# The sample's attention A made in 18 steps inside the gate stage, and one gate tile moved with it

## The reference, cut to what matters

```python
k_all = concatenate([cache_a_k, ka]); v_all = concatenate([cache_a_v, va])     # 2048 + 64 keys
logits = einsum(q, k_all) * 128 ** -0.5 + bias_a[t5_bucket(s_pos - t_pos)] + mask
oa = softmax(logits) @ v_all
m = sigmoid(ga) * ((oa * silu(za)) @ w_br_a) + sigmoid(gb) * ((ob * silu(zb)) @ w_br_b)
y = rmsnorm(x + m @ w_out, final_g)
```

## Time and profile before

| | us |
|---|---|
| median of 3 runs | 3204.95 (3204.02 to 3206.44) |
| profiled execution, its own time | 3202.53 |
| span of that execution | 3200.8 |
| TensorE busy in the span | 3049.3 (95%) |
| mean granted TensorE clock | 0.979 |
| `gates`, first to last product | 1473.7 to 2113.2 |
| last product of `attend_merge` to first of `merge_a` | 2492.6 to 2588.5 |

### The profile page before, as it was taken

The page is one execution under the profiler, slowest core; times in us unless marked ns, Lnnn a source line. Parts: engine busy times, 40 slices in busy tenths (PEclk is TensorE's granted clock), DMA queues, the critical chain, the costliest instruction groups (busy, mean ns, idle before and its releaser), DMA issues. The chain is left out here.

```text
span 3200.8 us, 46226 instructions
## 1 busy us (share of the span) xinstructions
PE 3049.3 (95%) x17703; PEld 2721.6 (85%) x17725; DVE 1408.1 (44%) x2351; ACT 950.0 (30%) x1945; POOL 870.6 (27%) x626
## 2 busy tenths in 40 slices
PE   6999999999999999999999999969999779899997
PEld 5999898898989889998999999868888579788875
DVE  6005457475658169601545545025555432220422
ACT  5112222313231121112334333125555331121422
POOL 1222211121212212222322322214444122233453
PEclk9999999999999999999999999979999789999998
DMA  4452232222222323333343343245332355453443
GB/s 159 113 132 66 75 79 61 73 68 69 74 64 70 82 53 101 96 83 94 108 117 106 108 116 97 59 143 161 118 111 69 85 190 193 155 210 111 145 162 105
DMA packets 386126, 342.31 MB, mean 107 GB/s; under 512 B 40208, under 2 KB 340784, under 8 KB 382432
## 3 DMA queue, kind: packets, MB, share of 16 engines
q1 hardware_dynamic: 365872, 276.32, 30.3%
q10 hardware_dynamic: 20080, 63.57, 6.0%
HBM read 252.07 MB, written 87.80 MB: 106 GB/s over the span
## 5 line engine op out<-in xcount | busy, mean ns | idle before, releaser
L538 POOL TENSOR_TENSOR w_in_tile_lo<-w_in_tile_raw,w_in_tile_hi 128x512 fp32r<-128x512 f32 x228 | 298.7, 1310 | 1139.8 <-ACT w_in_tile_hi L558 1139.8
L655 PE MATMUL banks<-h_hi,w_in_tile_hi 128*128 128x288 f32 (+3 forms) x2576 | 584.3, 332 | 0.7 <-PEq L134 0.7
L655 PE MATMUL banks<-h_lo,w_in_tile_hi 128*128 128x288 f32 (+3 forms) x2576 | 581.7, 331 | 0.0
L655 PE MATMUL banks<-h_hi,w_in_tile_lo 128*128 128x288 f32 (+3 forms) x2576 | 581.6, 331 | 0.0
L655 PEld LDWEIGHTS banks<-h_hi,w_in_tile_lo 128*128 128x128 f32 (+1 forms) x2576 | 441.0, 188 | 35.5
L655 PEld LDWEIGHTS banks<-h_lo,w_in_tile_hi 128*128 128x128 f32 (+1 forms) x2576 | 441.0, 188 | 35.4
L655 PEld LDWEIGHTS banks<-h_hi,w_in_tile_hi 128*128 128x128 f32 (+1 forms) x2576 | 436.5, 188 | 35.3 <-issue 1.6
L558 ACT CAST w_in_tile_hi<-w_in_tile_raw 128x512 fp32r<-128x512 f32 x228 | 141.6, 621 | 961.3 <-PE banks L655 957.0
L820 DVE MAX8 top<-score 128x8 f32<-128x384 f32 (+6 forms) x224 | 247.1, 1103 | 32.9 <-DVE score L823 0.9
L1227 PE MATMUL banks<-h_hi,w_in_tile_hi 128*128 128x288 f32 (+1 forms) x1056 | 233.6, 330 | 10.2 <-PEq L134 5.5
L823 DVE MATCH_REPLACE8 score<-top,score 128x384 f32<-128x384 f32 (+6 forms) x224 | 242.9, 1084 | 0.0
(11 more groups left out here) (254 smaller groups left out, 4529.0 us busy)
## 6 DMA issues: line engine op xcount, KB each, us to landing
w_in_tile_raw<-in_w_in SPq DMA_DIRECT2D x312, 256.0 KB, 2.9
w_out_tile_raw<-in_w_out SPq DMA_DIRECT2D x128, 256.0 KB, 2.5
product<-spill ACTq DMA_DIRECT2D x48, 544.0 KB, 3.4
product<-g_spill ACTq DMA_DIRECT2D x22, 544.0 KB, 2.9
g_q_raw<-product SPq DMA_DIRECT2D x68, 128.0 KB, 2.8
am_work<-product SPq DMA_DIRECT2D x16, 544.0 KB, 4.2
merged_b<-am_work ACTq DMA_DIRECT2D x16, 544.0 KB, 3.5
ma_gate_in<-product SPq DMA_DIRECT2D x16, 544.0 KB, 5.1
```

The costliest lines, as they stand in the source:

```text
L538: pool.tensor_tensor(s.w_lo[:, q, :, :], s.w_raw[:, q, :, :], s.w_hi[:, q, :, :].bitcast(F32), ALU.subtract).then_inc(lo_made, 1)
L655: last = pe.matmul(ps[0:m, 3 * slot + c, 0:w], w_[:, q, kq, 0:m], h_[:, k, t0:t0 + w], start=(k == 0 and w_ is s.w_hi and h_ is s.h_hi), s ...
```

## The change

`attend_a` is no longer called (the function is gone). Its work stands in `gates`, in steps `t = p - FIRST` of one piece each, with `FIRST = 2 * (34 + 3) = 74`: it begins behind the last unit of attention B, in the banks and in the SBUF of branch B. `gates` gets one tile more (`GATES_EARLY` 10 to 9, so 23 tiles and 92 pieces) and `project` one fewer; steps `t` = 0 to 17 are pieces 74 to 91.

For each of the two key heads `kv`, six steps apart: key chunk `c` is transposed in the middle of piece `t = 6 kv + c` (c = 0 to 3), the logits of a chunk are made at the start of the next piece (own keys at place 0), softmax stands in the steps in between, chunk `c` of the probabilities is turned at the start of `t = 6 kv + 6 + c` and multiplied by its values one piece later. So head 0 is turned in the pieces in which head 1's logits are made. The mask and the near table are added by VectorE as it moves the logits out, in place of the identity products. Keys, masks and values come in chunks, loaded by SyncE in the same steps.

```diff
-GATES_EARLY = 10
+GATES_EARLY = 9
@@ gates, SyncE: in step i, for p in (2i, 2i+1): sample_loads(p - FIRST), behind load_piece(2i+5), load_piece(2i+6)
+            def load_mask(kv, c):
+                if c == 0:
+                    sp.wait_ge(near_made, kv + 1)
+                elif c > 0:
+                    sp.wait_ge(taken, 2 * (PER_KV * kv + c + 1))
...
+            def load_k_cached(kv, c):
+                if kv or c:
+                    sp.wait_ge(sk_turned, CACHED * kv + c)
+                sp.dma_start(sk_raw[:, :, :], cache_ak[0, 0, 512 * c:512 * (c + 1), kv, :].rearrange(
+                    "(b p) d -> p b d", p=P)).then_inc(sk_in, 16)
...
+            def sample_loads(t):
+                if t == -2:
+                    sp.dma_start(far[0:DEC, :], rel_bias[N_BUCKETS // 2 - 1, 0:H_A:2].partition_broadcast(DEC), ...
...
+                for kv, c in kvs_at(t, 1, CACHED - 1):
+                    load_k_cached(kv, c + 1)
+                    load_mask(kv, c + 1)
+                for kv, _ in kvs_at(t, 4, 1):
+                    if kv + 1 < KV_A:
+                        load_k_cached(kv + 1, 0)
+                for kv, c in kvs_at(t, 5, PER_KV):
+                    load_values(kv, c)
@@ gates, GpSimd: in step i
                 split_lo(2 * i + 3)
                 if exists(n + 1):
                     scale_probs(n + 1)
+                sample_step(2 * i - FIRST)          # near_masked at t = -1, 5; values_lo at t = 6 .. 16
                 split_lo(2 * i + 4)
+                sample_step(2 * i + 1 - FIRST)
@@ gates, ScalarE: in step i
+                sample_turned(2 * i - FIRST)        # copies the turned probabilities, two banks
                 if i and i % 2 == 0:
                     evacuate(i // 2 - 1)
...
                 split_hi(2 * i + 3)
...
+                sample_step(2 * i - FIRST)          # q_hi, values_hi, exps, k_hi
+                sample_turned(2 * i + 1 - FIRST)
                 split_hi(2 * i + 4)
+                sample_step(2 * i + 1 - FIRST)
@@ gates, VectorE: behind the branch-B work of step i, for p in (2i, 2i+1)
+            def take_sample(kv, place):
...
+                        last = dve.scalar_tensor_tensor(out=sprob[:, u, cols.start:cols.start + n0], in0=bank[:, 0:n0], scalar=f,
+                                                        in1=mask[:, 0:n0], op0=ALU.add, op1=ALU.add)
...
+                dve.tensor_reduce(chunk_max[:, :, place], sprob[:, :, cols], AX.X, ALU.max).then_inc(chunk_top, 1)
...
+            def sample_step(t):
+                for kv, c in kvs_at(t, 6, PER_KV):
+                    turned_lo_sample(kv, c)
+                for kv, place in kvs_at(t, 0, PER_KV):
+                    take_sample(kv, place)
+                for kv, _ in kvs_at(t, PER_KV, 1):
+                    scale_sample(kv)
+                for kv, _ in kvs_at(t, -1, 1):
+                    q_lo_sample(kv)
+                for kv, c in kvs_at(t, 0, CACHED):
+                    k_lo_sample(kv, c)
+                for kv, _ in kvs_at(t, 6 + PER_KV, 1):
+                    gate_sample(kv)
@@ gates, TensorE
+            def logits_sample(kv, place):
...
+                for u in range(2):
+                    if j:
+                        pe.wait_ge(taken, 2 * (j - 1) + u + 1)
+                    for q_, k_ in ((sq_hi, keys[0]), (sq_hi, keys[1]), (sq_lo, keys[0])):
+                        last = pe.matmul(ps[:, LOGITS + u, 0:w], q_[:, u * P:(u + 1) * P], k_[:, :], ...
...
+            def sample_step(t):
+                for kv, c in kvs_at(t, 7, PER_KV):
+                    meet_sample(kv, c)              # 3 products of 256 columns for each of 4 blocks of keys, 1 for own keys
+                for kv, c in kvs_at(t, 6, PER_KV):
+                    turn_sample(kv, c)              # 2 units, 4 transposes each, 1 for own keys
+                for kv, place in kvs_at(t, 0, PER_KV):
+                    logits_sample(kv, place)
             def piece(p):
+                sample_step(p - FIRST)
                 tile, q = p // 4, p % 4
                 if q == 0 and tile:
                     pe.wait_ge(evacuated, tile)
...
                 for kq in range(KQ):
                     k = q * KQ + kq
+                    if kq == KQ // 2:
+                        for kv, c in kvs_at(p - FIRST, 0, CACHED):
+                            turn_keys(kv, c)        # 4 transposes
@@ build
-        attend_a(nc, s, True, ins["cache_a_v"][0, 0], ins["cache_a_k"], outs["s_a_v"][0, 0], ins["rel_bias"])
```

More of the change, by code:

```diff
@@ new lines, in gates @@
+        sk_raw, sz, sk_hi, sk_lo, own_raw, own_lo, own_hi, near, few, mask, sq_raw, sq_lo, sq_hi, sprob, spt_hi, spt_lo, \
+            sv_raw, sv_lo, sv_hi = (t[x] for x in (
+                "k_raw", "z", "k_hi", "k_lo", "own_raw", "own_lo", "own_hi", "near", "few", "mask", "q_raw", "q_lo", "q_hi",
+                "prob", "pt_hi", "pt_lo", "v_raw", "v_lo", "v_hi"))
+        far, chunk_max = few[:, 0:4], few[:, 4:14].rearrange("p (u c) -> p u c", u=2)
+        sneg, stotal, sinv = few[:, 14:16], few[:, 16:18], few[:, 18:20]
@@ new lines, in gates, with kvs_at, key_cols, row_of @@
+        sv_in = semaphores(nc, ctx, "sa_v_in0", "sa_v_in1")
+        block = ctx.block()
+        def kvs_at(t, first, count):
+            return [(kv, t - first - kv * KV_STEP) for kv in range(KV_A) if 0 <= t - first - kv * KV_STEP < count]
+        def key_cols(kv, c):
+            if c < CACHED:
+                return slice(DEC + 512 * c, DEC + 512 * (c + 1))
+            return slice(0, DEC) if kv else slice(DEC + PAST, 2 * DEC + PAST)
+        def row_of(kv):
+            return slice(0, DEC + PAST) if kv else slice(DEC, 2 * DEC + PAST)
@@ L883, in exists, with key_blocks @@
+        def key_blocks(c):
+            return [(k, P) for k in range(4)] if c < CACHED else [(0, DEC)]
         def exists(n):
@@ new lines, in load_near @@
+            def load_near(kv):
+                if kv:
+                    sp.wait_ge(taken, 2 * PER_KV * kv)
+                else:
+                    sp.wait_ge(summed, len(units))
+                for half in range(2):
+                    sp.dma_start(near[DEC * half:DEC * (half + 1), :, :],
+                                 shifted_lines(s, 4 * kv + half, DEC, 2, 2, OWN_W)).then_inc(near_in, 16)
+            def load_mask(kv, c):
[3 more added lines that the diff above has]
+                    sp.wait_ge(taken, 2 * (PER_KV * kv + c + 1))
+                elif kv:
+                    sp.wait_ge(taken, 2 * PER_KV * kv)
+                cols = slice(PAST - P, PAST + DEC) if c < 0 else slice(512 * c, 512 * (c + 1))
+                for half in range(2):
+                    sp.dma_start(mask[DEC * half:DEC * (half + 1), 0:cols.stop - cols.start], s.masks[SEQ:T, cols]).then_inc(
+                        mask_in, 16)
@@ new lines, in logits_sample @@
+            def logits_sample(kv, place):
+                j = PER_KV * kv + place
+                if place == 0:
+                    pe.wait_ge(sq_made, kv + 1)
+                    pe.wait_ge(own_made, kv + 1)
+                    keys, w = (own_hi, own_lo), DEC
+                else:
+                    pe.wait_ge(sk_made, CACHED * kv + place)
+                    keys, w = (sk_hi, sk_lo), 512
+                if j == 0:
+                    pe.wait_ge(summed, len(units))
+                for u in range(2):
+                    if j:
+                        pe.wait_ge(taken, 2 * (j - 1) + u + 1)
+                    for q_, k_ in ((sq_hi, keys[0]), (sq_hi, keys[1]), (sq_lo, keys[0])):
+                        last = pe.matmul(ps[:, LOGITS + u, 0:w], q_[:, u * P:(u + 1) * P], k_[:, :],
+                                         start=q_ is sq_hi and k_ is keys[0], stop=q_ is sq_lo)
+                    last.then_inc(slogits, 1)
```

641 lines of the change are left out of this document (232 added, 409 removed).

## The result

The changed kernel takes 3159.73 us (median of 4 runs, 3158.53 to 3161.64), where the kernel before, run beside it, took 3205.16: a ratio of 0.9855 with a 95% interval of 0.9843 to 0.9867, 45.4 us less. The forecast was 3158 (46.7 less, from a median of 3204.95), with a range of 3152 to 3174. The profiled execution took 3158.93 us, with a span of 3157.1 us and a mean granted clock of 0.983.

A forecast was written before the change was run, and what follows sets the result against it. TensorE was taken as the bound nearly throughout, except in the sample's stage, a path of links between engines. Stage removed -81.7, TensorE work moved in +34.4, emptying +0.6: -46.7 us from 3204.95, so 3158 us, range 3152 to 3174.

The forecast's parts named there:

- Part 1: Sample's own stage before `merge_a`: 95.9 us between products go, less a 14.2 us handover that stays: -81.7 us.
- The handover put together from two halves: Wait between `attend_merge` and `merge_a`: 3.3 us from last product to first load plus 10.9 to first product, 14.2 us.
- rival 2: Emptying of accumulators hidden after all and handover to `merge_a` shorter: 3154 us; chance 0.05 with anything faster still.
- Part 2: Tile moved from `project` to `gates`: same products, so it costs nothing net; its emptying is counted separately.
- Part 3: TensorE work moved into `gates`: keys 3.2, logits 12.5, probabilities 6.7, values 12.0, charged by pitches only: +34.4 us.
- Part 4: TensorE's waits in the moved steps: links have time to spare; emptying accumulators 4.4 us against 3.8 before: +0.6 us.
- The rule against it: Softmax in `gates`: VectorE and GpSimd block each other; scalings could lose 3.4 us against 3.0 spare, sum -46.3.
- rival 3: Moved stretch of `gates`: TensorE pauses in each step and falls to 1.2 GHz, +141.7 us, 3300; chance 0.03.
- The sum: Whole kernel: -81.7 + 34.4 + 0.6 = -46.7 us, from a median of 3204.95 to 3158 us.

The follow-up runs named there:

- two extra scalings: Changed kernel with two more scalings by 1.0 on VectorE, each waited for, ahead of each of the four real ones: 3164.3 us, ratio 0.9863.
- one pass of values: Changed kernel with one of three passes in the product of probabilities and values, low halves not multiplied: 3151.20 us, ratio 0.9826.
- keys at the start: Changed kernel with the keys turned at the first contraction step of the piece, not in its middle: 3160.58 us, ratio 0.9854.
- four extra scalings: Changed kernel with four more scalings by 1.0 on VectorE, each waited for, ahead of each of the four real ones: 3177.71 us, ratio 0.9911.
- masks first: Changed kernel with SyncE loading each step's mask ahead of the cached key chunk (t = 1 to 3 of each head): 3180.57 us, ratio 0.9917.

## Why the prediction was right, point by point

**Part 1, the stage that goes.** 81.7 us forecast, 81.3 in the profiled execution, 81.7 by the trace of the kernel without the stage, 85.0 (82 to 90) by its median; the last is not explained. The handover put together from two halves, 14.2 us, measured 14.5 to 14.7 in the three traces of the changed kernel. It was not shorter, so rival 2 lost that half.

**Part 2, the moved tile at nothing.** Alone it gave a ratio of 1.0007 (0.9998 to 1.0016), which holds nothing and the 1.3 us of its emptying, visible as the sixth wait, and can't tell them apart.

**Part 3, TensorE's work.** The forecast of parts 3 and 4 together was 34.4 us and +0.6 us against the kernel before. Against a gate stage with its 23 tiles and nothing in them the sample's steps cost 34.3 us. For that comparison the forecast is 34.4 less 0.7, since four bare tile starts wait 5.1 us and 4.4 were forecast; the 35 us expected of the kernel without the sample's attention left this out. So 33.7 stand against 34.3, and this hides two small misses of opposite sign. In the bare stage the waits for the emptying are 6.0 us, in the changed kernel 4.0, so 34.3 is 36.3 of TensorE's time less 2.0 of cover. The 36.3 are 1.9 over the sum by pitches. The step that was a little short is "with no gap as groups change, so I charge pitches only": it holds for the changes in those rows, and not behind transposes. In the whole stretch the first triple behind a key turn takes 0.57 to 0.58 us (8 times) and behind turned probabilities 0.57 to 0.61 (5 times), where 0.50 is usual, and the first of the 512-column logits behind turned probabilities 0.32 (4 times), where 0.23 is. These 17 places give 1.4 us. The products with the values of the sample's own 64 keys, two groups of three, add about 0.4, and a few other changes the rest. Two steps read in full were 0.06 and 0.12 us longer than worked out (7.81 for 7.75 at `t = 1`, 10.08 for 9.96).

**Part 4, the waits.** Forecast at the four tile starts (`t` = 2, 6, 10, 14) 0, 1.6, 0.5 and 2.3 us, 4.4 in all; measured 0, 1.2, 0.1 and 1.9, about 3.2. The mechanism (ScalarE's written order puts two turned banks ahead of the accumulators) is shown by the kernel that swaps them. The sizes were off by 0.4 each at `t = 6` and 14, from both sides: ScalarE was done 2.8 and 4.3 us into the step, not 3.1 and 4.5 (two banks take 1.07 us, not 2 x 0.59), and TensorE's own work ended at 1.6 and 2.5 us, not 1.5 and 2.2. So the net is 4.0 against 4.7 before, -0.7 rather than +0.6. Softmax had 3.4 and 4.6 us to spare, against 3.0 and 3.6, and the scalings show where that ends. The key loads took 3.2 us at the median for 256 KB, as the weight tiles' 3.0 had suggested and not as the 7.8 of the 512 KB loads; TensorE never waited for them.

**The rule against it.** The delay that it warns of is there. In the changed kernel GpSimd's low half of 128 x 512, 1.3 us elsewhere, took 2.12 us beside VectorE's second scaling, and VectorE's query half of 256 columns 1.52 us beside GpSimd; the same query half took 0.42 in the kernel with two extra scalings.

```profile
2040.22 2.12 POOL L1155 TENSOR_TENSOR w_in_tile_lo<-w_in_tile_raw,w_in_tile_hi 128x512 fp32r<-128x512 f32 x1 [6.70 <-ACT w_in_tile_hi L1213]
```

In all three traces of the changed kernel the four scalings themselves kept their 1.32 us, so softmax paid nothing. In the kernel with two extra scalings the first real scaling of each head was the one to wait; that of head 0:

```profile
2041.39 2.23 DVE L1470 TENSOR_SCALAR sa_prob<-sa_prob,sa_few 128x2112 f32<-128x2112 f32 x1
```

That is 0.9 us more, beside a GpSimd instruction from 2041.20 to 2042.50. The trace agrees with the Trainium skill ("SBUF — State Buffer", "Who interferes with whom"); in these rows the engine that began second is the one that took longer, and beside the scalings of the changed kernel that was GpSimd, whose halves are wanted two pieces later. The forecast charged nothing for the rule, and nothing was paid; that the scalings began first was not worked out beforehand.

**The clock (rival 3).** It stayed at 1.00 through the moved stretch. The longest pause was 1.88 us, as forecast not over 2.3. But the reasoning was weaker than the outcome: behind the same 1.88 us the clock was down in two of the experiments, so a pause under 2.3 us is no safe one. The stake was small, as there is only one such pause and the fall behind it (0.83 over 10 us) cost 1.7 us.

**The sum.** Of the profiled executions -43.7, forecast -46.7. The gate stage accounts for +2.2 of the difference (60.9 for 23.7 + 34.4 + 0.6 = 58.7), the handover for 0.4, `attend_merge` for 0.9, the stages behind it for 1.1; the segment ahead of `gates` gave 1.6 more than the 23.7 that a tile costs (its length differs by 3.3 us between three traces of the changed kernel). Of the +2.2, the start of `gates` is a part: its first 10 us had a clock of 0.71 in this execution and 0.84 in the one before, 1.3 us, and a second execution of the changed kernel has 0.84 too. In medians it is -45.4 in the first set of executions, -49.5 and -48.9 in the two later ones, so -46.7 lies among them and is not known better than to some 2 us. The forecast was right by its own steps; the errors are each under 2.5 us and partly cancel, and that part of the closeness is luck.

## What to carry to other kernels

A dependent chain that had the core to itself can cost nothing but its TensorE time, if it is cut into steps of one piece each and every link has a whole step: here 81 us of stage became 34 us of products, and VectorE, ScalarE and GpSimd took their parts for free. Count the products by their pitch and add about 0.1 us for the first product behind each run of transposes, then check each link's spare time, since a link that is only 2 us late can be paid a second time through the clock. In a queue that serves several links, put the load that is wanted first ahead of any that has to wait for this step's work: swapping two lines cost half the gain.

## What the runs showed of the hardware

- **A pause of about 2 us may take the clock or may not.** The same wait of 1.88 us for the emptying at `t = 14` left the clock of the 10 us behind it at 1.00 in six traces (the changed kernel three times, one pass of values, keys at the start, two extra scalings) and at 0.83 in two (four extra scalings, masks first), though TensorE's products just before and behind it are the same. The two had other pauses of 5.55 and 2.87 us ahead of it, 21 and 39 us before; in the six the pause before, of 1.23 or 0.31 us, is 19 us or more away. In the kernel with the masks first, pauses of 2.21, 2.27 and 2.11 us were followed by 1.00, those of 2.76 and 2.73 by 0.83 and 0.85, and the longest, 2.87, by 1.00 again. In the kernel with two extra scalings a pause of 1.88 us, 1.6 us of work and a pause of 0.82 us went with a fall to 0.50 that lasted until 2055.9. So the length of one pause alone does not decide it; what else does, the pauses ahead or chance, stays open. Two of these stretches, kernel with the masks first:

```profile
2070.40:2080.40 10.00, 10.00 (x57) 9.22 (x58) 2.94 (x5) 2.70 (x5) 1.20 (x1) 0.83 0.21 58
...
2099.53:2109.53 10.00, 9.85 (x61) 8.71 (x62) 4.22 (x9) 3.69 (x9) 1.71 (x2) 1.00 0.45 143
```

- **How long TensorE stays at 1.2 GHz behind the same pause varies between executions.** The first 10 us of `gates`, behind 5.5 to 5.8 us of idle, had mean clocks of 0.71, 0.79 and 0.84 in three traces of the changed kernel, 0.69 with the tile moved alone, 0.84 and 0.74 in the kernel before with and without its stage: up to 1.5 us, without any difference in the code of that stretch. `attend_merge` varied more, 366.8 to 372.0 us; in the four traces in which it took 370.0 us or more its third 20 us have a clock of 0.86 to 0.91, in the others read for it 0.96 to 1.00. The four are both of the kernel that empties first, the tile moved alone, and the kernel before without its stage; what decides it stays open. It may be why a gain of 4 us that both traces show in one stage can be missing in a median.
- **Two copies in a row cost less than twice one.** ScalarE's two turned banks took 1.07 us, one alone 0.59; VectorE's two differences of 0.69 took 1.29.
- **A first product behind transposes costs more; behind most other changes it does not.** From start to start a triple of 288 columns takes 0.57 to 0.58 us behind the key turns and 0.50 behind most logits, and a product of 512 columns 0.32 us behind turned probabilities and 0.23 behind a piece. Four of the ten triples behind logits took 0.58 to 0.60 all the same; three of these are the first of a tile.
